# Hybrid decoder layer on one core: compression weights loaded in the projection's last pass, position products first, rows turned a head ahead

## The reference, cut to what matters

```python
def compress(kv, pos_emb, w1, w2):
    # kv (B,S,G,dh) -> (B,Nc,G,dh): overlapping blocks (length 32, stride 16) -> one token each
    n_c = (S - CMP_BLOCK) // CMP_STRIDE + 1                       # 127
    idx = jnp.arange(n_c)[:, None] * CMP_STRIDE + jnp.arange(CMP_BLOCK)[None, :]
    blocks = kv[:, idx] + pos_emb[None, None, :, None, :]
    flat = blocks.transpose(0, 1, 3, 2, 4).reshape(B, n_c, G, CMP_BLOCK * dh)
    return jax.nn.gelu(flat @ w1) @ w2

kc = compress(k_cmp, cmp_pos[0], cmp_w1[0], cmp_w2[0])
vc = compress(v_cmp, cmp_pos[1], cmp_w1[1], cmp_w2[1])
```

## Time and profile before

| what | value |
|---|---|
| median of 3 runs | 3850.33 us (3845.58 to 3852.93) |
| the profiled execution, its own time | 3852.21 us |
| its span, first to last instruction | 3850.4 us |
| granted clock of PE, mean (1.0 is full) | 0.944 |
| PE busy | 3510.7 us, 91% of the span |
| projection | 0 to 416.4 us |
| compression | 416.4 to 497.7 us |

### The profile page before, as it was taken

The page is one execution under the profiler, slowest core; times in us unless marked ns, Lnnn a source line. Parts: engine busy times, 40 slices in busy tenths (PEclk is TensorE's granted clock), DMA queues, the critical chain, the costliest instruction groups (busy, mean ns, idle before and its releaser), DMA issues. The chain is left out here.

```text
span 3850.4 us, 55869 instructions
## 1 busy us (share of the span) xinstructions
PE 3510.7 (91%) x19064; PEld 2999.8 (78%) x19064; DVE 2376.6 (62%) x5054; ACT 1796.1 (47%) x3061; POOL 1251.5 (33%) x1951
## 2 busy tenths in 40 slices
PE   6999757989898999999989889599999999999997
PEld 6999646878787888888868768478888888888876
DVE  9999245666666667766774244476564666666354
ACT  3333125666666776776677333233332333333232
POOL 5454024444443333323322023433231235332031
PEclk9999769999999999999899989799999999999998
DMA  4343220000000000000000045332224452322344
GB/s 145 117 144 120 70 52 27 24 17 16 16 16 16 16 13 11 9 14 5 7 9 4 34 154 163 131 110 80 92 81 148 166 178 77 110 99 85 140 142 148
DMA packets 189764, 289.62 MB, mean 75 GB/s; under 512 B 33458, under 2 KB 129842, under 8 KB 189490
## 3 DMA queue, kind: packets, MB, share of 16 engines
q1 hardware_dynamic: 188004, 283.97, 22.0%
q10 hardware_dynamic: 1488, 2.20, 0.2%
HBM read 211.15 MB, written 74.97 MB: 74 GB/s over the span
## 5 line engine op out<-in xcount | busy, mean ns | idle before, releaser
L1459 ACT ACTIVATE a_p_t<-a_ps_st 128x512 f32<-128x512 f32 x716 | 437.7, 615 | 370.8 <-PE a_ps_st L1349 192.3
L2482 PE MATMUL f_ps<-f_x_hi,f_w_hi 128*128 128x512 f32 x1232 | 482.7, 392 | 37.2 <-DVE f_w_lo L2603 37.2
L1466 ACT ACTIVATE a_junk_a<-a_index,a_tk 128x384 bf16<-128x384 f32 (+13 forms) x336 | 445.2, 1325 | 112.2 <-DVE a_halves L1576 56.1
L2482 PE MATMUL f_ps<-f_x_lo,f_w_hi 128*128 128x512 f32 x1232 | 481.8, 391 | 0.0
L2482 PE MATMUL f_ps<-f_x_hi,f_w_lo 128*128 128x512 f32 x1232 | 481.6, 391 | 0.0
L1375 PEld LDWEIGHTS a_ps_o<-a_vsl,a_p_t 128*128 128x128 f32 x2176 | 316.9, 210 | 25.4 <-DVE a_fin L1673 2.3
L1180 POOL TENSOR_SCALAR a_tk<-a_tk,a_halves 128x1 f32<-128x1 f32 x336 | 104.0, 309 | 630.0 <-ACT a_junk_a L1466 628.8
L1375 PE MATMUL a_ps_o<-a_vsl,a_p_t 128*128 128x65 f32 x2176 | 299.9, 285 | 1.4 <-DVE a_fin L1673 1.4
L2482 PEld LDWEIGHTS f_ps<-f_x_hi,f_w_hi 128*128 128x128 f32 x1232 | 232.9, 189 | 87.5 <-DVE f_w_lo L2603 39.2
L1375 PEld LDWEIGHTS a_ps_o<-a_dv,a_p_t 128*128 128x128 f32 x2176 | 288.6, 193 | 8.8
L2502 PE MATMUL f_ps<-f_w_hi 128*128 128x512 f32 x704 | 275.1, 391 | 4.8 <-DVE f_w_lo L2613 4.8
(11 more groups left out here) (327 smaller groups left out, 8467.1 us busy)
## 6 DMA issues: line engine op xcount, KB each, us to landing
f_raw<-in_w_down SPq DMA_DIRECT2D x88, 512.0 KB, 3.3
px_raw<-in_x_t SPq DMA_DIRECT2D x48, 512.0 KB, 4.4
f_raw<-in_w_gate SPq DMA_DIRECT2D x44, 512.0 KB, 4.7
f_raw<-in_w_up SPq DMA_DIRECT2D x44, 512.0 KB, 4.5
g_scratch<-f_gs SPq DMA_DIRECT2D x22, 1024.0 KB, 7.5
f_raw<-g_scratch SPq DMA_DIRECT2D x88, 256.0 KB, 3.4
z_scratch<-p_z SPq DMA_DIRECT2D x16, 768.0 KB, 3.4
o_scratch<-a_oacc SPq DMA_DIRECT2D x32, 256.0 KB, 2.1
```

The lines of the kernel that those rows point to most:

```text
L1459: act.activation(p_t[:, s % PT_RING, :], ps_st[s % ST_BANKS][:, :], ACT.Exp, scale=SCALE).then_inc(exp_done, 1)
L1466: act.activation(junk_a[:, 0:w], index[t % 2][:, 0:w], ACT.Sign, bias=thr, scale=-1.0, accum_out=cnt).then_inc(counted, 1)
L2482: mm = pe.matmul(out[:, :], w[:, j, k * P:(k + 1) * P], x[:, j, k], start=(k == 0 and i == 0), stop=(k == 3 and i == 2))
```

## The change

The raw weight buffer of the projection becomes a tensor `shared` that outlives the projection. In step 18 (the third step of pass 3) SP issues seven transfers of what the compression needs into it: the two halves of `w1`, `pos`, `w2k` twice, `w2v` and the identity. PE waits for all seven once, at the start of the compression. The four transfers of rows are issued by SP (heads 0 and 2) and ACT (heads 1 and 3). On PE the position products come first, then turn 0, turn 1, hidden 0, turn 2, hidden 1, turn 3, hidden 2, hidden 3. The cosine table is held once and read with a repeat, which takes one activation away.

```diff
@@ projection_phase
-        w_raw = sb("pw_raw", [P, 4, 4, WMAX])
+        w_raw = shared[:, 0:16 * WMAX].rearrange("p (b k n) -> p b k n", b=4, k=4)
-        cos2 = sb("p_cos", [P, TILES, 2, 12])
+        cos1 = sb("p_cos", [P, TILES, 12])
...
+                if N == NS - PAIRS_Q + 2:
+                    sp.wait_ge(w_lo_done, SEVEN * PASSES)
+                    for dst, src in cmp_in:
+                        sp.dma_start(dst, src).then_inc(cmp_ld, 16)
                 if N >= 1:
                     store(N - 1)
...
-                    act.activation(cos2[:, :, 0, :], rr[:, 1], ACT.Sin).then_inc(trig_done, 1)
-                    act.activation(cos2[:, :, 1, :], rr[:, 1], ACT.Sin).then_inc(trig_done, 1)
+                    act.activation(cos1[:, :, :], rr[:, 1], ACT.Sin).then_inc(trig_done, 1)
...
+def compression_loads(shared, cmp_pos, cmp_w1, cmp_w2, ident_in):
+    w1, w2k, w2v, pos, ident = compression_weights(shared)
+    return [(w1[:, b], cmp_w1[b].rearrange("(c p) n -> p c n", p=P)) for b in range(2)] + [
+        (pos, cmp_pos), (w2k[:, 0], cmp_w2[0]), (w2k[:, 1], cmp_w2[0]), (w2v, cmp_w2[1]), (ident, ident_in)]
@@ compression_phase, sync
-            sp.dma_start(ident[:, :], ident_in).then_inc(ident_ld, 16)
-            for h in range(4):
+            for h in (0, 2):
                 sp.dma_start(rows[:, :, h, 0, :], ...).then_inc(rows_ld[h], 16)
-            sp.dma_start(pos[:, :, :], cmp_pos).then_inc(w_ld, 16)
@@ compression_phase, tensor
+            pe.wait_ge(cmp_ld, 16 * 7)
+            for b in range(2):
+                for c in range(LC):
+                    mm = pe.matmul(small[:, b:b + 1], w1[:, b, c], pos[:, b, c:c + 1], start=(c == 0), stop=(c == LC - 1))
+            mm.then_inc(small_full, 1)
+            turn(0)
+            turn(1)
+            hidden(0)
+            turn(2)
+            hidden(1)
+            turn(3)
+            hidden(2)
+            hidden(3)
@@ compression_phase, scalar
-            for b in range(2):
-                act.dma_start(w1[:, b], cmp_w1[b].rearrange("(c p) n -> p c n", p=P)).then_inc(w_ld, 16)
-            for twice in range(2):
-                act.dma_start(w2k[:, twice], cmp_w2[0]).then_inc(w_ld, 16)
-            act.dma_start(w2v[:, :], cmp_w2[1]).then_inc(w_ld, 16)
+            for h in (1, 3):
+                act.dma_start(rows[:, :, h, 0, :], z_rows[:, :, head_col[h]:head_col[h] + HEAD]).then_inc(rows_ld[h], 16)
@@ compression_phase, vector
-                if n == 4:
+                if n == 3:
                     dve.wait_ge(small_full, 1)
                     dve.tensor_copy(posb[:, :], small[:, 0:2]).then_inc(v, 1)
```

More of the change, by code:

```diff
@@ L77, with projection_phase @@
 PI_MAX = float(np.nextafter(np.float32(np.pi), np.float32(0)))
-def projection_phase(nc, x_t, w_in, b_in, pos, inv_freq, z):
+def projection_phase(nc, x_t, w_in, b_in, pos, inv_freq, z, shared, cmp_in, cmp_ld):
     NS = PASSES * PAIRS_Q
@@ L418, in summed @@
                     if N == 0:
-                        dve.wait_ge(trig_done, 4)
+                        dve.wait_ge(trig_done, 3)
                     op = dve.tensor_tensor(zt[:, u, 1, w:2 * w], u3, piece, ALU.add)
@@ L439, in rope @@
                 zr = zt[:, N % 2, i, 0:heads * dim].rearrange("p (h d) -> p h d", h=heads)[:, :, 0:2 * f].rearrange("p h (a f) -> p h a f", a=2)
-                cs = cos2[:, tile, :, fo:fo + f].unsqueeze(1).broadcast_to([P, heads, 2, f])
+                cs = cos1[:, tile, fo:fo + f].unsqueeze(1).unsqueeze(1).broadcast_to([P, heads, 2, f])
                 sn = sin2[:, tile, :, fo:fo + f].unsqueeze(1).broadcast_to([P, heads, 2, f])
@@ L479, in _, with compression_weights, compression_phase @@
             rope(NS - 1, 0)
-def compression_phase(nc, z, cmp_pos, cmp_w1, cmp_w2, ident_in, kc, vc):
-    LC = CMP_BLOCK // 2
+LC = CMP_BLOCK // 2
+CMP_COLS = 2 * LC * P + 2 * HEAD + HEAD + 2 * LC + P
+def compression_weights(shared):
+    at, parts = 0, []
+    for n in (2 * LC * P, 2 * HEAD, HEAD, 2 * LC, P):
+        parts.append(shared[:, at:at + n])
+        at += n
+    w1, w2k, w2v, pos, ident = parts
+    return (w1.rearrange("p (b c n) -> p b c n", b=2, c=LC), w2k.rearrange("p (a d) -> p a d", a=2), w2v,
+            pos.rearrange("p (b c) -> p b c", b=2), ident)
+def compression_loads(shared, cmp_pos, cmp_w1, cmp_w2, ident_in):
+    w1, w2k, w2v, pos, ident = compression_weights(shared)
+    return [(w1[:, b], cmp_w1[b].rearrange("(c p) n -> p c n", p=P)) for b in range(2)] + [
+        (pos, cmp_pos), (w2k[:, 0], cmp_w2[0]), (w2k[:, 1], cmp_w2[0]), (w2v, cmp_w2[1]), (ident, ident_in)]
+def compression_phase(nc, z, shared, cmp_ld, kc, vc):
     LAST = CMP_STRIDE * (N_CMP - 1)
@@ L507, in compression_phase @@
         small = ctx.enter_context(nc.psum_tensor("c_small", [P, 512], F32))
-        ident_ld = sem("c_ident_ld")
-        w_ld = sem("c_w_ld")
         rows_ld = [sem(f"c_rows_ld{h}") for h in range(4)]
@@ L538, in _, with turn @@
         def _(pe):
-            pe.wait_ge(ident_ld, 16)
-            for h in range(4):
+            def turn(h):
                 pe.wait_ge(twice_done, h + 1)
@@ L551, in _, with hidden @@
                     mm.then_inc(turned_full, 1)
-                if h == 0:
-                    pe.wait_ge(w_ld, 16 * 6)
-                    for b in range(2):
-                        for c in range(LC):
-                            mm = pe.matmul(small[:, b:b + 1], w1[:, b, c], pos[:, b, c:c + 1], start=(c == 0), stop=(c == LC - 1))
-                    mm.then_inc(small_full, 1)
+            def hidden(h):
                 pe.wait_ge(upper_done, 4 * (h + 1))
@@ L2737, in layer @@
     ident = ap["consts"][:, CCOL["ident"]:CCOL["ident"] + P]
-    projection_phase(nc, ap["x_t"], ap["w_in"], ap["b_in"], ap["pos"], ap["freq"], z)
     with ExitStack() as ctx:
@@ L2741, in layer @@
         vc = ctx.enter_context(nc.sbuf_tensor("vc", [P, GROUPS, CV], F32))
-        compression_phase(nc, z, ap["cmp_pos"], ap["cmp_w1"], ap["cmp_w2"], ident, kc[:, :, :], vc[:, :, 0:HEAD])
+        with ExitStack() as early:
+            shared = early.enter_context(nc.sbuf_tensor("shared", [P, 16 * max(WIDTHS)], F32))
+            cmp_ld = early.enter_context(nc.semaphore("cmp_ld"))
+            cmp_in = compression_loads(shared, ap["cmp_pos"], ap["cmp_w1"], ap["cmp_w2"], ident)
+            projection_phase(nc, ap["x_t"], ap["w_in"], ap["b_in"], ap["pos"], ap["freq"], z, shared, cmp_in, cmp_ld)
+            compression_phase(nc, z, shared, cmp_ld, kc[:, :, :], vc[:, :, 0:HEAD])
         attention_phase(nc, z, ap["consts"], kc[:, :, :], vc[:, :, :], o_mix)
```

## The result

The changed kernel takes 3829.76 us (median of 5 runs, 3828.85 to 3834.58), against 3851.83 for the kernel before (5 runs, 3845.58 to 3853.34). The ratio is 0.9945 with a 95% interval of 0.9934 to 0.9956, which is a gain of 17 to 25 us. A later pair of the same two kernels (experiment 11) gave 0.9954 (0.994 to 0.9967). The prediction was 3831.4 us, between 3826 and 3839, and 18.7 us of gain in the compression.

What follows compares the result with a forecast made beforehand. The compression was taken as one chain on PE; 9.80 + 6.16 + 0.56 + 2.18 = 18.7 us off the median of 3850.33 gave 3831.6, or 3831.4 us with half of turn 1's possible clock rise, range 3826 to 3839.

Steps and rivals of the forecast that it cites:

- Which wait bounds the phase: Compression: a single chain on PE gives the whole phase, 81.23 us before and 62.5 us after the change.
- Start to position products: Compression's start: PE begins position products 0.10 us after the phase's start instead of waiting 9.90 us; gain 9.80 us.
- Turn 0: First turn, after the position products: its rows are ready and turn 1 follows at once, 3.93 us for 10.09; gain 6.16.
- Turn 1: Second turn: 3.54 us at half clock with no wait behind it, for 4.10; gain 0.56, or 1.09 if the clock has risen.
- Turns 2 and 3: Later turns: the idle time of 1.09 us ahead of hidden 2 and of hidden 3 goes; gain 2.18 us.
- The early loads at 0: Projection, step 18: SP's issue of seven transfers takes 2.4 to 13.6 us, taken near the lower, and costs the kernel 0.
- 5 us more do nothing: Projection, step 19: DVE's sum is already 2.4 us late, and 5 us more would not delay PE.
- The cosine table at 0: Kernel's start: one activation less on ACT, 0.25 us, behind which ACT idles 2.45 us for POOL; gain 0.
- Rows by two queues: Compression's row loads: at 21 ns a packet heads 0 and 1 land near 424, the others by 429.5, ahead of need.
- the rival of late rows: Compression: interleaved transfers bring head 0 only with head 1, turn 0 starts at 432.3; gain 16.5, time 3833.8; chance 8%.
- Position products at full clock: Rival, compression: unbroken work lifts PE's clock early, products shrink to 8.9 or 6.8 us; gain 24.0, time 3826.3; chance 6%.
- The size of the whole: Whole kernel: 18.7 us of gain in the compression passes on, for 3831.4 us.

Runs made afterwards that it cites:

- experiment 11: The changed kernel unchanged, run again beside the kernel before: 3834.87 us, ratio 0.9954 to the kernel before.
- 6: The changed kernel unchanged, in one more profiled execution: compression 62.15 us.
- Experiment 2: The changed kernel with each head's turn right before its own hidden product, position products still first: phase 65.65 us.
- experiment 4: The changed kernel with four more 1 MB transfers ahead of the seven in step 18: compression starts at 421.32 in place of 416.56.
- experiment 7: The changed kernel with all position products moved to the end of the projection's program on PE: 3829.16 us, ratio 0.9941 to the kernel before.
- experiment 9: The changed kernel with each position product 64 columns wide, the position column repeated: 3831.49 us, ratio 0.9949 to the kernel before.
- experiment 1: The changed kernel with PE's order of before, early loads and two queues of rows kept: 3840.6 us, ratio 0.997 to the kernel before.

## Why the prediction was right

- **Which wait bounds the phase.** Right: one chain on PE. The phase was put at 62.5 us and took 62.0, 62.2 and 61.7.
- **Start to position products** (9.80). They start at 416.57, at the barrier, and take 13.46 us until the first transpose (13.61 in the sum), at clock 0.50.
- **Turn 0** (6.16). It starts at 430.03, forecast 430.15, with no gap, and turn 1 follows 434.15 - 430.03 = 4.12 later (3.93 in the sum): the first pair of groups took 2.16, not 1.97.
- **Turn 1** (0.56, or 1.09 if the clock has risen). 437.20 - 434.15 = 3.05 us, so the gain was 1.05, near the upper of the two values. It came there by another way than a turn at full clock: its first eight transposes still took the 1.57 us of half clock, and only the last eight ran at full (0.42 for four), since the clock rose at about 435.7. In experiments 11 and 6 it rose at 434.7 and 436.8, and turn 1 took 2.77 and 3.22; that 3.05 is so near 3.01 is luck. It makes up for the 0.19 above, and with the 0.15 of the products most of the half microsecond between 62.5 and 62.0.
- **Turns 2 and 3** (2.18). No wait ahead of hidden 2 and 3. Experiment 2 prices all of the turning ahead at 3.65.
- **The early loads at 0.** The verdict was right, the size of the issue was not: I took a value near 2.4 us, and it was 10.4, near the upper bound of 13.6. The step did not rest on that size, since the slack was also counted at the upper bound. The slack held: the sum of step 19 started at 347.57, and of the 11.3 us that it was held up in experiment 4, 8.4 passed before PE stood idle, where I had "5 us more do nothing".
- **The cosine table at 0.** No run isolates it. The compression starts 0.12 us later than before, so it brought nothing that shows.
- **Rows by two queues.** Head 0 was doubled by 423.2, before its need at 430.15; the rival of late rows fell. The 5.5 us worked out from 21 ns a packet are near for the pair: doubling starts 5.6 and 6.8 us after the phase's start, the second at 423.39 where I had 424, and the last head's at 427.97 where I had 429.5.
- **Position products at full clock.** Fell: the clock was 0.50 from 416.56 to 430. Experiments 7 and 9 go further: one-column products lost a full clock that PE had, and products of 64 columns did not win it. Its price was off too: 13.61 us became 8.9 there by the ratio of the transposes, where 64 records at the measured 116 ns are 7.4.
- **The size of the whole.** The chain gives 81.2 - 62.0 = 19.2 us; the measured ratios give 21 and 18 with intervals of 8 and 10 us that hold it. Of the 4.1 us that the first pair of profiles differs beyond the phase, 2.6 lie in the attention, within its scatter; the rest was not followed.

## What to carry to other kernels

A phase between two barriers is priced best by the starts of the rows on its one chain; such a sum held to half a microsecond here, where the whole kernel's runs differ by 8. Constants of the next phase belong into a buffer that is already dead in this one, but count what stands behind them in the queue: issuing took 10 us, and only the slack of a store made it free. Then look for idle time of the bound engine on the other side of the barrier: half of the position products there gave another 6.6 us of the phase, while all of them gave nothing, since they outlasted both the idle time and the full clock. A kernel's clock at such a place is not the same in every execution, so look at more than one profile before counting on it.

## What the runs showed of the hardware

- 32 position products (64 records) ran in unbroken work and PE lost its full clock under them, at about 413.6 (experiment 7), no later than where PE stood idle (412.9 to 415.6). The Trainium skill ("TensorE: Matmul & The Clock Gate", Part 1) has sustained matmul work release the throttle; for these products, 13.7 us of them at 0.50 in the kernel before, the changed one and experiment 1, and 64 columns wide too (experiment 9), it did not.
- The clock rose from 0.50 to 1.00 under two kinds of work. Where two turns follow the products, it rose under the float32 transposes (in the changed kernel between 435 and 436, with transposes from 430.03). In the kernel before, turn 0 left it at 0.50 (426.34 to 430, then idle time), and in experiment 1 turn 0 with products behind it did so too; in these two it rose only near the end of the first hidden product, at about 456 and 446.
- A record of a one-column float32 product costs 116 ns at 2.4 GHz and 216 at 1.2; the hidden product with its strided operand costs nearly the same at both (6.8 and 6.9 us). In experiment 2 the clock fell to 0.50 for some 3 us under an unbroken hidden product, which took 6.78 us all the same.
